# The mixer's output projection as a block product of seven, with two operands' rests on VectorE

## What is computed

```python
    yz = (y_ssd * jax.nn.silu(z_ssd)).reshape(bsz, length, SSD_GROUPS, D_MIX_SSD // SSD_GROUPS)
    y_ssd = rmsnorm(yz, ssd_norm.reshape(SSD_GROUPS, -1)).reshape(bsz, length, D_MIX_SSD)
    v = causal_dwconv(sc_c * sc_h, sc_conv_w)
    y_sc = sc_b * v * jax.nn.silu(z_sc)

    mix = jnp.concatenate([y_ssd, y_sc], axis=-1) @ w_out
    x = x + rmsnorm(mix, norm_post)

    gate = jax.nn.sigmoid(x @ w_ple_gate)
    return x + gate * (p_i @ w_ple_proj)
```

## Time and profile before

| | us |
|---|---|
| median of 3 runs | 2393.75 (2391.98 to 2397.63) |
| the profiled execution | 2392.79 |
| its span | 2391.0 |
| TensorE busy | 2318.7 (97%) |
| VectorE busy | 1582.6 (66%) |
| GpSimd busy | 1166.3 (49%) |
| ScalarE busy | 889.7 (37%) |
| the projection, from the span's start | 625.1 to 801.5 |

### The profile page before, as it was taken

How to read it: one execution, slowest core, us unless ns; L and a number is a source line. 1 busy time by engine, 2 the same in 40 slices (tenths; PEclk the granted TensorE clock), 3 DMA queues, 4 the chain that set the end, 5 groups by cost and what they waited for, 6 DMA issues and landing times.

```text
span 2391.0 us, 33033 instructions
## 1 busy us (share of the span) xinstructions
PE 2318.7 (97%) x12306; PEld 1881.6 (79%) x12306; DVE 1582.6 (66%) x2066; ACT 889.7 (37%) x1383; POOL 1166.3 (49%) x699
## 2 busy tenths in 40 slices
PE   7999999999999998999999999999999999999996
PEld 5787777778888786778878777888777888788885
DVE  6657878876611648435776676656787666876788
ACT  4455464442200324553423323222363333434344
POOL 4355667663443535445233333334465545566664
PEclk9999999999999999999999999999999999999997
DMA  5323333337111353333122222222135444844221
GB/s 214 132 103 113 130 125 108 128 126 262 44 44 53 116 138 118 132 119 129 57 67 70 85 73 66 81 95 70 62 124 181 145 150 154 337 187 169 96 106 71
DMA packets 130087, 285.73 MB, mean 120 GB/s; under 512 B 13601, under 2 KB 49441, under 8 KB 125362
## 3 DMA queue, kind: packets, MB, share of 16 engines
q1 hardware_dynamic: 96672, 230.61, 27.5%
q10 hardware_dynamic: 33298, 53.56, 6.9%
HBM read 205.43 MB, written 78.72 MB: 119 GB/s over the span
## 4 chain that ended last, share of the span: by engine, by line
PE 45%; DVE 8%; issue 3%; DMA 2%; ACT 2%; POOL 1%; DVEq 0%; SPq 0%; ACTq 0%
PE pt L3744 15%; PE pt L3215 11%; PE wk L3744 6%; PE wk L3571 4%; PE pt L3571 3%; DMA eb<-o_d 1%; PE wk L3755 1%; PE wk L3656 1%; DVE darg L2750 1%; PE pt L3231 1%; DVE eb L2832 1%; PE wk L3694 1%; PE wk L3690 1%; PE wk L3689 1%; DVE ea L2834 0%
## 5 line engine op out<-in xcount | busy, mean ns | idle before, releaser
L834 POOL TENSOR_TENSOR w_hi<-w_raw,ones 128x1024 fp32r<-128x1024 f32 x70 | 136.8, 1954 | 542.0 <-PE pt L3215 503.3
L838 POOL TENSOR_TENSOR w_lo<-w_raw,w_hi 128x1024 fp32r<-128x1024 f32 x80 | 217.3, 2716 | 86.7 <-ACT w_hi L1110 65.5
L896 POOL TENSOR_TENSOR xl<-sraw,xh 128x512 fp32r<-128x512 f32 x80 | 137.6, 1730 | 81.0 <-ACT xh L1180 79.7
L979 POOL TENSOR_TENSOR wr_l<-raw,wr_h 128x512 fp32r<-128x512 f32 x80 | 137.0, 1718 | 81.2 <-ACT wr_h L1802 81.2
L3215 PE MATMUL pt<-h,w_hi 128*128 128x512 f32 x512 | 168.1, 409 | 0.0
L3215 PE MATMUL pt<-l,w_hi 128*128 128x512 f32 x512 | 158.5, 391 | 0.0
L3215 PE MATMUL pt<-h,w_lo 128*128 128x512 f32 x512 | 158.2, 390 | 0.0
L949 POOL TENSOR_TENSOR l<-kq,h 128x512 fp32r<-128x512 f32 x64 | 89.2, 1404 | 102.5 <-ACT h L1484 102.5
L979 POOL TENSOR_TENSOR wr_l<-fraw,wr_h 128x512 fp32r<-128x512 f32 x60 | 80.1, 1339 | 91.4 <-ACT wr_h L1802 91.4
L3215 PE MATMUL pt<-xh,w_hi 128*128 128x512 f32 x384 | 119.5, 393 | 0.6 <-ACT ea L1366 0.6
L3215 PE MATMUL pt<-xh,w_lo 128*128 128x512 f32 x384 | 118.7, 390 | 0.0
(11 more groups left out here) (669 smaller groups left out, 6726.1 us busy)
## 6 DMA issues: line engine op xcount, KB each, us to landing
w_raw<-ws_d SPq DMA_DIRECT2D x82, 512.0 KB, 3.4
fx_d<-stg SPq DMA_DIRECT2D x106, 256.0 KB, 2.8
sraw<-ws_d SPq DMA_DIRECT2D x32, 512.0 KB, 5.8
fraw<-ws_d SPq DMA_DIRECT2D x32, 512.0 KB, 5.0
raw<-ws_d SPq DMA_DIRECT2D x32, 512.0 KB, 8.6
kq<-ws_d SPq DMA_DIRECT2D x14, 1024.0 KB, 5.5
xs0f<-fx_d SPq DMA_DIRECT2D x10, 1024.0 KB, 4.9
xs1f<-fx_d SPq DMA_DIRECT2D x9, 1024.0 KB, 4.8
```

The source lines that it names most:

```text
L834: nc.gpsimd.tensor_tensor(out=w_hi[:, u, :], in0=w_raw[:, u, :], in1=zeros, op=ALU.add).then_inc(w_hi_done, 1)
L838: nc.gpsimd.tensor_tensor(out=w_lo[:, u, :], in0=w_raw[:, u, :], in1=w_hi[:, u, :].bitcast(f32), op=ALU.subtract).then_inc(w_split, 1)
L896: nc.gpsimd.tensor_tensor(out=lo, in0=sc_factor(n, SC_ORDER[i]), in1=hi.bitcast(f32), op=ALU.subtract).then_inc(sw_lo, 1)
L979: nc.gpsimd.tensor_tensor(out=low, in0=src, in1=high.bitcast(f32), op=ALU.subtract).then_inc(wl_done, 1)
```

## The change

The projection becomes a product of 2 x 2 blocks with seven block products where there were eight. The blocks are: of the weights, the two inputs (`y_sc`, `y_ssd`) by two halves of the output features; of the operands, the two inputs by two token halves. A block product is four weight tiles of 128x1024 on operands of 8 x 128x512, 24 matmuls a tile: 28 tiles g = 0 to 27, in the order 1, 2, 6, 7, 4, 5, 3 (`O_ORDER`), one PSUM bank each.

- Operands: VectorE makes T1 to T4 out of the token halves (`operand_sum`, 32 instructions of 128x512), ScalarE rounds them (`operand_high`), VectorE makes the rests: `operand_low` for T2, T4 and T1, `third_low` for T3 and `branch_low` for the block B22 (8 instructions each). The last two are what the change's name speaks of. The sums T1 and T3 of rows 0 to 5 are put ahead of `branch(7)` on VectorE, those of rows 6 and 7 behind the rests of the first input.
- Weights: for products 6, 7, 5 and 3 the tile is a sum or difference of two or three tiles (`weight_sum`, VectorE). ScalarE rounds each tile (`o_high`), and GpSimd makes only its rest (`o_rest`). Loads: 28 raw ones (`o_load`) into the two `w_raw` buffers, and the further tiles (`o_load_more`): 8 for product 6, 4 each for 7, 5 and 3. There are four buffers for finished tiles; the rounding of g waits until TensorE has done tile g-4.
- Outputs: ScalarE copies bank after bank (`first_copy` to `last_copy_21`), VectorE adds the banks in `wk` to the copies (`block_sum`, 12), and squares go by halves of 128x512 (16 on ScalarE, 16 additions on VectorE).
- The residual's first-half rows stand between the last weight sums on VectorE; the gate's weight rest `weight_low` stands behind `square_sum(15)`; the residual's input loads of the first half stand between the last weight loads of SyncE.

The core of the diff:

```diff
+O_ORDER = (1, 2, 6, 7, 4, 5, 3)
+O_TILES = 4 * len(O_ORDER)
...
+        def o_load(g):
+            i, q = divmod(g, 4)
+            if g < 2:
+                sp.wait_ge(w_split, S_SB + 7 + g)
+            else:
+                sp.wait_ge(o_lo, O_LO + g - 1)
+            tile = O_FIRST + 2 * q + {1: 0, 2: 1, 6: 0, 7: 0, 4: 9, 5: 9, 3: 1}[O_ORDER[i]]
+            sp.dma_start(o_raw(g), halves(ws[tile, :, :])).then_inc(o_raw_in[g % 2], 16)
+
+        def o_load_more(g):
...
+            if O_ORDER[i] == 5:
+                sp.wait_ge(o_prod, O_PROD + 16)
+                sp.dma_start(o_kept(q), halves(ws[m1_s, :, :])).then_inc(o_ext_in[q], 16)
+                return
+            sp.wait_ge(o_prod, O_PROD + g - 3)
+            if O_ORDER[i] == 6:
+                sp.dma_start(hi, halves(ws[m1_s, :, :])).then_inc(o_ext_in[q], 16)
+                sp.dma_start(lo, halves(ws[m1_y, :, :])).then_inc(o_ext_in[q], 16)
+            elif O_ORDER[i] == 7:
+                sp.dma_start(lo, halves(ws[m1_s, :, :])).then_inc(o_ext_in[q], 16)
+            else:
+                sp.dma_start(lo, halves(ws[m0_s, :, :])).then_inc(o_ext_in[q], 16)
...
+        for g in range(10):
+            o_load(g)
+        for g in range(8, O_TILES):
+            if g < 16:
+                o_load_more(g)
+            if g >= 24:
+                if g < 26:
+                    for k in range(4 * (g - 24), 4 * (g - 24) + 4):
+                        x_load(0, k)
+                o_load_more(g)
+            if g + 2 < O_TILES:
+                o_load(g + 2)
+            if g == 18:
+                for q in range(4):
+                    o_load_more(20 + q)
...
-        before_norm(S_GATE)
-        lows(xl, xres, xh, KT, 3 * KT)
+        def o_rest(g):
+            hi, lo = o_slot(g)
+            pool.wait_ge(o_hi, O_HI + g + 1)
+            nc.gpsimd.tensor_tensor(out=lo, in0=o_factor(g), in1=hi.bitcast(f32), op=ALU.subtract).then_inc(o_lo, 1)
...
+        def o_high(g):
+            i, q = divmod(g, 4)
+            if g < 4:
+                act.wait_ge(*((mm_done, S_SB + 7), (stat_done, 3), (mm_done, S_OUT), (mm_done, S_OUT))[g])
+            else:
+                act.wait_ge(o_prod, O_PROD + g - 3)
+            if O_ORDER[i] in (6, 7, 5, 3):
+                act.wait_ge(o_wsum, O_WSUM + o_sums_before(g) + 1)
+            else:
+                act.wait_ge(o_raw_in[g % 2], O_RAW_IN + 16 * (g // 2 + 1))
+            A(o_slot(g)[0], o_factor(g), ACT.Copy).then_inc(o_hi, 1)
...
+        def third_low(k):
+            dve.wait_ge(o_th, O_TH + O_HIGH.index(("T3", k)) + 1)
+            TT(out=sl[:, k, cols(1)], in0=vbuf[:, k, cols(1)], in1=xl[:, k, cols(0)].bitcast(f32), op=ALU.subtract).then_inc(o_lp, 1)
...
+        def weight_sum(g):
+            i, q = divmod(g, 4)
+            hi, lo = o_slot_raw(g)
+            raw = o_raw(g)
+            dve.wait_ge(o_raw_in[g % 2], O_RAW_IN + 16 * (g // 2 + 1))
+            dve.wait_ge(o_ext_in[q], O_EXT_IN[q] + {6: 32, 7: 48, 5: 64, 3: 80}[O_ORDER[i]])
+            if O_ORDER[i] == 6:
+                link(TT(out=hi, in0=hi, in1=lo, op=ALU.add))
+                ins = TT(out=raw, in0=hi, in1=raw, op=ALU.subtract)
+            elif O_ORDER[i] == 7:
+                ins = TT(out=raw, in0=raw, in1=lo, op=ALU.subtract)
...
+        for k in range(6):
+            operand_sum("T1", k)
+            operand_sum("T3", k)
         branch(7)
...
+        for k in range(KT):
+            second_input_low(k)
...
+        for k in range(4, KT):
+            operand_sum("T2", k)
+            operand_sum("T4", k)
+            operand_low("T2", k - 4)
+        block_sum("C11", 0)
+        weight_sum(8)
+        for k in range(4, KT):
+            operand_low("T2", k)
+        weight_sum(9)
...
+        weight_sum(12)
+        for k in range(KT):
+            third_low(k)
+        for g in range(13, 16):
+            weight_sum(g)
...
+        def mixer_tile(g, between=None):
...
+            pe.wait_ge(o_lo, O_LO + g + 1)
...
+        mixer_tile(21, between=lambda k: mixer_sums(0, (o_acc, O_ACC + KT)) if k == 1 else None)
+        mixer_tile(22, between=lambda k: mixer_spread(0) if k == 1 else None)
```

More of the change, by code:

```diff
@@ L856, in split_pairs @@
                     rest(u, j * 2 + u + 1)
[L858 to L871, removed]
         def difference_lo(i):
@@ L1398, in mixer_out @@
[L1398 to L1408, removed]
@@ L1409, in _ @@
-        mixer_out(KT - 2, 0, slice(0, T), [(mm_done, S_OUT + 2 * KT - 2)]).then_inc(evac_done, 1)
-        mixer_out(KT - 1, 1, cols(0), [(half_mm, 1)]).then_inc(half_ev, 1)
+        branch_copy(6)
+        o_high(0)
+        branch_high(6)
+        o_high(1)
+        branch_copy(7)
+        o_high(2)
+        branch_high(7)
+        for k in range(KT):
+            second_input(k)
+        o_high(3)
+        o_high(4)
+        for k in range(4):
+            operand_high("T3", k)
+        o_high(5)
@@ new lines, in _ @@
+        first_copy(0)
+        for k in range(4, KT):
+            operand_high("T3", k)
+        first_copy(1)
+        o_high(6)
+        first_copy(2)
+        o_high(7)
+        first_copy(3)
+        for k in range(6):
+            operand_high("T2", k)
+        o_high(8)
+        operand_high("T2", 6)
+        operand_high("T2", 7)
+        o_high(9)
+        o_high(10)
+        for k in range(KT):
+            operand_high("T4", k)
+        o_high(11)
+        second_copy(0)
+        o_high(12)
@@ new lines, in _ @@
+        for k in range(4):
+            operand_high("B22", k)
+        second_copy(1)
+        o_high(13)
+        for k in range(4, KT):
+            operand_high("B22", k)
+        second_copy(2)
+        o_high(14)
+        second_copy(3)
+        for k in range(4):
+            operand_high("T1", k)
+        o_high(15)
+        for k in range(4, KT):
+            operand_high("T1", k)
+        third_copy(0)
+        o_high(16)
+        third_copy(1)
+        o_high(17)
+        square_of("C11", 0)
@@ L1412, in residual_high @@
+        square_of("C11", 1)
+        third_copy(2)
+        o_high(18)
+        square_of("C11", 2)
+        square_of("C11", 3)
+        third_copy(3)
+        o_high(19)
+        for q in range(4):
+            last_copy_21(q)
+            o_high(20 + q)
         def residual_high(q):
@@ L1432, in _ @@
         weight_high(S_GATE)
-        for q in range(3, 10):
+        for q in range(KT, 10):
             residual_high(q)
@@ L2408, in weight_low @@
+        for k in range(KT):
+            operand_low("T1", k)
+        for k in range(KT):
+            branch_low(k)
+        for n in range(4):
+            square_sum(n)
+        weight_sum(20)
+        weight_sum(21)
+        square_sum(4)
+        weight_sum(22)
+        square_sum(5)
+        weight_sum(23)
+        square_sum(6)
+        square_sum(7)
         def weight_low(S):
@@ L3462, in _ @@
         pair(3, S_SB, N_SB, (xh, xl))
[L3464 to L3471 removed]
         def mixer_sums(h, ready):
             pe.wait_ge(*ready)
[L3475 removed]
+            for c in range(4 * h, 4 * h + 4):
+                ins = MM((bank(0), wk[:, 3, :])[h][:, c:c + 1], acc_a[:, c * P:(c + 1) * P], ones[:, 0:1], start=True, stop=True)
```

387 lines of the change are left out of this document (314 added, 73 removed).

## The result

The changed kernel takes 2443.31 us (median of four, 2436.96 to 2451.55) against 2395.21 on the same chip (2391.98 to 2397.63): a ratio of 1.0204 (1.0170 to 1.0237), 48 us slower. The forecast was 2432, with 2415 to 2446 as its range.

What follows compares the result with a forecast made beforehand. TensorE, busy for 97% of the span, was taken to bound the kernel. On the profiled 2392.8 us, -21.8 + 9.0 + 36.9 + 12.7 + 2 = +38.8 gave 2431.6, 2432 on the median, range 2415 to 2446.

Steps and rivals of the forecast that it cites:

- Part 1: Projection matmuls: 768 become 672, 28 tiles of 24 at 5.44 us each; -21.8 us.
- Part 2: Projection start: twelve operand sums ahead of row 7 make TensorE wait 7.4 us, then run slow matmuls; +9.0 (3 to 11).
- the ring: From tile 8: rest of g, loads for g+1, sum, rounding, rest of g+1, without overlap; 12.45 or 9.8 us a turn.
- Part 3: Weight sums of products 6 and 7: loads waiting for GpSimd's rests delay TensorE through tile 15; +36.9 us (+33 to +43).
- Part 4: Products 4 and 5: a tile is ready each 4.0 us, so TensorE runs through; cost 0, up to 3 us.
- Part 5: Product 3: loads wait behind rests again, with residual loads among them, delaying tiles 25 to 27; +12.7 us (8 to 17).
- Part 6: Way into the gate: VectorE's rest of the gate's second tile stands behind the last block sum and square; +2 (0 to 5).
- the stages behind are bound by TensorE and pass the delay on: After the projection: later stages add no delay of their own; no term in the sum.
- (a): Tiles 9 to 15: shared SBUF access of VectorE and GpSimd, not loads, sets the pace; +4.7 there, 2387 us; chance 0.07.
- (b): Projection: all added work is hidden, the start too; -21.8, 2371 us; chance 0.02.
- (c): The ring exists but its turns are nearer to 8 us; 2400 to 2415 us; chance 0.07.
- (d): TensorE kept at 1.2 GHz well beyond products 6 and 7, another 38 us in products 4 and 5; 2470 us; chance 0.04.

Runs made afterwards that it cites:

- row7_early: Changed kernel with only one of the six T1/T3 sum pairs left ahead of branch row 7 on VectorE: 2442.4 us, ratio 1.0188 to the kernel before.
- ahead67: Changed kernel with SyncE issuing the further tiles of g+1 ahead of raw tile g+2's load in products 6 and 7: 2409.7 us, ratio 1.0053.
- rests_gpsimd: Changed kernel with the 16 rests of T3 and B22 made by GpSimd instead of VectorE: 2440.4 us, ratio 1.0184.
- all_three_gpsimd: Changed kernel with further tiles issued one tile early in products 6, 7 and 3, row 7 early, and T3's and B22's rests on GpSimd: 2401.9 us, ratio 1.0038.
- before_brow: Kernel before the change with the two small-packet transfers issued some 500 us earlier: 2392.4 us, ratio 0.9982.
- before: The kernel before the change, unedited: 2393 to 2398 us over the chips used, ratio 1.
- after_brow: Changed kernel with the two small-packet transfers issued some 500 us earlier: 2437.2 us, ratio 1.0175 to the kernel before.
- after: The changed kernel, first measurement and profile, against the kernel before: 2443.3 us, ratio 1.0204.
- again: The changed kernel run once more without an edit: 2444.0 us, ratio 1.0192 to the kernel before.
- reordered: Changed kernel with further tiles issued early, row 7 early, small packets early and VectorE's list reordered: 2390.3 us, ratio 0.9975 to the kernel before.

## Why the prediction was right, point by point

By the prediction's own parts, in the first profile (tiles counted from TensorE's first matmul of the projection at 627.75):

- **Part 1**, -21.8: the tiles of products 4 and 5 run at 5.44 us each. As said.
- **Part 2**, +9.0: TensorE waited 7.25 us in tile 0 for VectorE's row 7 (7.4 forecast) and started 12 matmuls 0.43 us apart behind that, which is 2.7 us late in all and not 1.6. Tile 8 began at 681.42, 53.7 us after tile 0 and not 43.5: +10.2. In the sum it may stand beside the ring's term, which is counted from 721.2, with these 9.0 in it. But it isn't worth 9 us by itself: row7_early took it away and got 0.3 us of stretch for it. The rest of tile 8 came at 678.4, which is 675.7 by the forecast's clock (674.5 forecast; TensorE began 2.6 us later here), 3 us before TensorE began the tile, and only because TensorE was already late. So the range, which lets the start fall to 3 while the ring stays at 33, was added up wrongly: with an early start the ring's term grows by what the start's shrinks.
- **Part 3**, +36.9: the mechanism is shown by the rows and by ahead67. The turns were 12.99, 12.77, 13.39 and then 10.17, 9.70, 9.67, 11.05, 79.7 us for the seven against 76.6. Tile 15 ended at 765.3, 83.9 us after tile 8's start instead of 43.5: +40.4. One term that was small is the three loads: 6.9 us from the first issue to VectorE's start in the turn shown, not 6.4. Another part of the text was off: it foresaw waits of about 7 and 4 us, and they were 4.4 to 4.8 and 2.3 to 3.7, since the forecast took a turn less 5.44 for them and left out the slow matmuls of its own Part 2: of each tile's 24, TensorE started 12 in tile 9, 14 in tile 10 and 7 or 8 in tiles 11 to 15 at 0.43 us. The sum didn't notice, since what a slow tile takes from the wait the ring takes back.
- **Part 4**, 0: tiles 16 to 23 took 46.5 us, 45.0 + 1.5; 0.58 of it is a wait at tile 24.
- **Part 5**, +12.7: mis-sized. From tile 24's first matmul (811.84) to the gate's (851.58) it was 39.7 us for 21.8 of work, +18.0, just over the upper bound of 17. The forecast gave tile 24 a lead of 3 us (ready at 800, due at 803). There was none: rest 23 came 14.9 us before tile 24 was due and not 17.1, and VectorE began the sum 9.3 us after that rest and not 7.9, so rest 24 (811.79) came as tile 24 was due. That is 3 of the 5.3 us. The turns were 14.66, 11.1 and 8.4 for 14, 11 and 7, the other 2. (The recorded 837.6 is a slip of 0.2: 832 + 5.4 is 837.4.)
- **Part 6**, +2: VectorE's rest made TensorE wait 1.69 us. But the gate's first part is 1.1 us shorter than before (29.8 against 30.9), since the clock stayed at 1.00 there and was 0.94. -1 and not +2.

The sum -21.8 + 10.2 + 40.4 + 1.5 + 18.0 - 1.1 = 47.2 stands against 46.4 in the stretch (253.7 - 207.3); the remainder is in 0.8 us that the projection of before lost to its own seams. The forecast's 38.8 was 7.6 low in the stretch: 3.5 by part 3, 5.3 by part 5 and 1 to 2 each by parts 2 and 4, less 3 in part 6 and the 0.8. Behind the stretch there were 8 us in the profiles that it didn't have at all; "the stages behind are bound by TensorE and pass the delay on" is the step that failed there. And 2.6 us of the first profile's span lay ahead of the projection and were absent in the repeat.

Of the rivals, (a) is refuted as the pace of this kernel by ahead67, though the lock itself is there: with the rings open it is part of what fills VectorE's list. The sentence under (a) that moving rests shortens only GpSimd's queue holds for the ring (rests_gpsimd), not without it: in all_three_gpsimd VectorE's adds got longer and the stretch grew by 6.3 us. (b) and (c) are out by the turns. (d) did not come true: the clock was 1.00 in products 4 and 5. The forecast's side and range held, the range narrowly: 2443.3 stands 3 us under its upper end, and the two distances of the profiles, 46.4 + 8.1 = 54.5 us, would have lain outside. So the mechanism was right by its rows, and that the number fell inside owes something to luck.

## What to carry to other kernels

When several operands of a step are loaded by one in-order queue, write down for each load which finished work it waits for and what stands behind it; a wait that cost nothing while each step needed one load becomes a closed ring when it needs three, and moving two lines of the issuing loop gave back 34 of 46 us. A wait isn't worth its length by itself: take one away alone and it can reappear at the next thing that the same engine's list is late for. And before trading matmuls for additions, add up the list of the engine that adds: here in the best order it filled two stages to 97%, and of 21.8 us saved at most 3.6 came through.

## What the runs showed of the hardware

- **Small packets on another queue hold up a large load.** Two transfers of 4 KB in packets of 4 bytes stretched a load of 512 KB on another queue, issued 2.3 us later, from 6.9 to 12.0 us in one kernel (before_brow, before) and from 8.3 to 20.1 and 21.9 in the other (after_brow, after and again; 17 to 20 in its variants). Why it is 12 here and 20 there stays open.
- **The clock falls within each tile of a ring.** After each idle time of 2.3 to 4.8 us TensorE started 7 to 14 matmuls of the tile's 24 at 0.43 us, the 1.2 GHz level, and the others at 0.23, so the granted clock was 0.82 over 84 us; it was 1.00 again in the tiles that followed without a wait. After a wait of 1.69 in the gate it didn't fall; in the kernel before it did after 1.93.
- **The lock between VectorE and GpSimd, once more.** In the turn above two rests of 128x512 took 3.08 us beside GpSimd's 2.40 (0.69 each without), as in the earlier trace rows. It goes both ways: in all_three_gpsimd GpSimd's rests of 128x512 took about 1.7 us each beside VectorE's adds, against 1.29 in the earlier trace rows. In reordered three sums of 128x512 took 4.25 us beside one GpSimd rest:

```profile
677.23 4.25 DVE L2676 TENSOR_TENSOR xbc<-xbc,mm 128x512 f32<-128x512 f32 x3
...
678.55 2.39 POOL L1057 TENSOR_TENSOR os_b_l<-w_raw,os_b_h 128x1024 fp32r<-128x1024 f32 x1 [4.78 <-ACT os_b_h L1551]
```
